# The last expert's rows of both routed MoE layers are added to the stream by a product on TensorE instead of a scatter and a read-back

## The reference

```python
# x (1, 512, 1024) behind 16 meta tokens: 528 rows of a stream h
h = h + short_conv_mixer(rmsnorm(h, a_norm), a_w_in, a_conv, a_w_out)
h = h + hier_moe(rmsnorm(h, ffn_norm[0]), ...)          # MoE layer 0, 528 rows
kv = rmsnorm(h, kv_norm) @ w_kv                         # keys and values from the stream
h = h[:, 16:]
h = h + diff_attention(rmsnorm(h, b_norm), ...)
h = h + hier_moe(rmsnorm(h, ffn_norm[1]), ...)          # MoE layer 1, 512 rows
return rmsnorm(h, final_norm)
# hier_moe: 32 experts in 4 groups; a row takes the 2 best experts of its best group
#   y = sum over the two: gate_k * (silu(x @ w_gate[e]) * (x @ w_up[e])) @ w_down[e]
```

## Time and profile before

| | us |
|---|---|
| median of 3 runs | 1638.5 |
| lowest, highest | 1637.38, 1640.2 |
| the profiled execution: its own time | 1636.99 |
| its span, first to last instruction | 1635.2 |

### The profile page before, as it was taken

How to read it: one execution, slowest core, us unless ns; L and a number is a source line. 1 busy time by engine, 2 the same in 40 slices (tenths; PEclk the granted TensorE clock), 3 DMA queues, 4 the chain that set the end, 5 groups by cost and what they waited for, 6 DMA issues and landing times. The chain is left out here.

```text
span 1635.2 us, 17518 instructions
## 1 busy us (share of the span) xinstructions
PE 1361.8 (83%) x6689; PEld 755.3 (46%) x6689; DVE 378.6 (23%) x729; ACT 341.0 (21%) x625; POOL 190.1 (12%) x314
## 2 busy tenths in 40 slices
PE   5999994999888888875999978895999888888882
PEld 4999772333322322233676755783333322323230
DVE  3434423000000000004431388623000000000003
ACT  5222220101000000004544366331010000000002
POOL 2000000111111111111000000001112111111111
PEclk9999995999999999997999979996999999999996
DMA  9120417999999999995312110317999999999994
GB/s 342 44 104 1 167 75 315 415 425 425 425 427 426 424 425 426 426 416 180 111 52 103 52 52 1 155 57 304 415 425 425 425 426 427 423 426 423 424 382 165
DMA packets 60922, 472.67 MB, mean 289 GB/s; under 512 B 10592, under 2 KB 10668, under 8 KB 35776
## 3 DMA queue, kind: packets, MB, share of 16 engines
q1 hardware_dynamic: 46480, 441.48, 65.2%
q0 software_dynamic: 14384, 30.36, 5.0%
HBM read 465.17 MB, written 23.13 MB: 299 GB/s over the span
## 5 line engine op out<-in xcount | busy, mean ns | idle before, releaser
L943 PE MATMUL ps<-ring,act 128*64 128x512 f32 x1792 | 443.8, 649 | 74.7 <-DMA ring<-in_e_up 68.8
L943 PEld LDWEIGHTS ps<-ring,act 128*64 128x64 f32 x1792 | 139.9, 142 | 373.9 <-issue 373.9
L910 PE MATMUL ps<-parts 128*128 128x512 f32 (+1 forms) x1104 | 265.1, 398 | 8.3 <-DVE parts L1220 7.7
L966 PE MATMUL ps<-ring,act 128*64 128x512 f32 x896 | 204.6, 597 | 31.0 <-ACT act L763 31.0
L1403 DVE TENSOR_TENSOR act<-act,ps 128x256 f32<-128x256 f32 x64 | 26.9, 421 | 870.1 <-ACT act L761 870.1
L910 PEld LDWEIGHTS ps<-parts 128*128 128x128 f32 (+1 forms) x1104 | 194.0, 178 | 69.1 <-DVE parts L1220 5.9
L896 PE MATMUL ps<-parts 128*128 128x264 f32 x1152 | 143.6, 287 | 4.5 <-DVE parts L1215 2.9
L896 PEld LDWEIGHTS ps<-parts 128*128 128x128 f32 x1152 | 142.3, 190 | 5.5 <-issue 5.5
L761 ACT ACTIVATE act<-ps 128x256 f32<-128x256 f32 x64 | 24.6, 384 | 574.3 <-PE ps L943 574.3
L966 PEld LDWEIGHTS ps<-ring,act 128*64 128x64 f32 x896 | 70.8, 136 | 126.2 <-issue 126.2
L1215 DVE TENSOR_TENSOR parts<-ring,parts 128x1024 fp32r<-128x1024 f32 x64 | 77.8, 1224 | 117.6 <-ACT parts L694 117.4
(11 more groups left out here) (163 smaller groups left out, 880.8 us busy)
## 6 DMA issues: line engine op xcount, KB each, us to landing
ring<-in_e_gate SPq DMA_DIRECT2D x56, 2048.0 KB, 18.2
ring<-in_e_up SPq DMA_DIRECT2D x56, 2048.0 KB, 22.5
ring<-in_e_down SPq DMA_DIRECT2D x56, 2048.0 KB, 22.4
arena<-in_e_down SPq DMA_DIRECT2D x8, 2048.0 KB, 15.6
ring<-in_a_w_in SPq DMA_DIRECT2D x6, 2048.0 KB, 19.6
arena<-in_e_up SPq DMA_DIRECT2D x6, 2048.0 KB
arena<-in_e_gate SPq DMA_DIRECT2D x6, 2048.0 KB
ring<-in_w_kv SPq DMA_DIRECT2D x4, 2048.0 KB, 13.2
```

What stands on the lines that cost most here:

```text
L910: last = mm(bank, x[:, k, :], w[:, k, :], start=(k == 0 and i == 0), stop=(k == KC - 1 and i == 2))
L943: last = mm(ps[f * C:(f + 1) * C, 2 + b, :].rearrange("p (g m i) -> p g m i", g=2, i=2), x, w, start=(k == 0), stop=(k == KC - 1))
L966: last = mm(ps[o * C:(o + 1) * C, 6 + b, :], hT[:, b, (2 * c + a) * C:(2 * c + a + 1) * C], w[:, f * D + o * DH:f * D + (o + 1) * DH], sta ...
```

## The change

The rows of expert 31 are no longer scattered and read back. After routing, DVE multiplies the slot marks of choices 0 and 1 by gate and by "this choice is expert 31", adds the two, and writes the 64 columns twice side by side (`hot_gate`). PE transposes that, DVE copies it into a free half of `nat`. ACT copies the last expert's result to `last_y` (two halves of the columns, on partitions 0 to 63 and 64 to 127). For each tile, PE multiplies the marks by the result (`add_last`, two products of 64 rows by 512 columns), and DVE adds the result to h (`take_last`). As no scatter writes those places of `expert_rows`, POOL fills all of them with zeros early in the kernel. The part for further blocks moves ahead of the last expert on every engine, and so does the read-back. ACT's squares of the two later norms are written elsewhere, as `nat` is occupied.

```diff
+        hot_gate = act17[:, 3584:4224].rearrange("p (t a n) -> p t a n", t=NX + 1, a=2)
+        def last_gate(t):
+            return nat[:, 0, DH + t * P:DH + (t + 1) * P] if t < NX else nat[:, 1, DH:DH + META]
+        def last_rows(layer, t):
+            b = 2 * (t % 2) if layer == 0 else 2 * t
+            return ps[0:rows(t), b:b + 2, :]
+        last_y = nat[:, 0, 0:DH]
+        def squares(phase, t):
+            return y_in(min(t, NX - 1), 0)[0:rows(t), :] if phase in (2, 4) else nat[0:rows(t), t % 2, :]
...
 POOL, start
+            nc.gpsimd.memset(zero, 0.0).then_inc(zero_ready, 1)
+            pool.wait_ge(zero_ready, 1)
+            pool.wait_ge(in_done, 6)
+            for l in range(2):
+                for k in range(2):
+                    for t in range(NX):
+                        pool.dma_start(y_dram[l][k * SPREAD + t * P:k * SPREAD + (t + 1) * P, :].rearrange("p (a n) -> p a n", a=2),
+                                       bcast(zero, 2, 1)).then_inc(zeroed, 16)
...
+            pool.wait_ge(zeroed, 16 * (4 * NX + 2))
 POOL, moe
+                        if last and u == 1:
+                            continue
                         pool.wait_ge(y_ready, E * layer + q * 2 + u + 1)
...
                 for b in range(2):
-                    pool.wait_ge(scattered[layer][b], 16 * PAIRS)
+                    pool.wait_ge(scattered[layer][b], 16 * (PAIRS - b))
 ACT, moe: pair(q, early) becomes one(q, u, early, final=False) for u in 0, 1
-                        if not first:
+                    if not first and not final:
                             act.wait_ge(scattered[layer][u], q * 16)
-                        nc.scalar.copy(y_out[:, u, :], ps[:, 6 + u, :]).then_inc(y_ready, 1)
+                    nc.scalar.copy(last_y if final else y_out[:, u, :], ps[:, 6 + u, :]).then_inc(y_ready, 1)
...
-                with act.Fori(EARLY, PAIRS) as q:
+                with act.Fori(EARLY, PAIRS - 1) as q:
                     pair(q, False)
+                one(PAIRS - 1, 0, False)
                 more = load_more(act, layer)
                 with act.If(more > 0):
...
+                one(PAIRS - 1, 1, False, True)
 PE, moe
+                pe.wait_ge(last_marked, layer + 1)
+                for t in range(nt):
+                    r = rows(t)
+                    at = ps[:, 4, t * P:(t + 1) * P] if t < NX else ps[:, 5, 0:META]
+                    last = nc.tensor.transpose(at, hot_gate[0:r, t, :, :].rearrange("p a n -> p (a n)"), ident[0:r, 0:r])
+                last.then_inc(last_turned, 1)
                 pe.wait_ge(gathered[layer][0], 16)
                 turn_block(0).then_inc(x_turned, 1)
...
-                pair(PAIRS - 1, False, True)
+                one(PAIRS - 1, 0, False, True)
                 more = load_more(pe, layer)
                 with pe.If(more > 0):
...
+                one(PAIRS - 1, 1, False, True)
 PE, after the layers
+            def add_last(layer, t):
+                pe.wait_ge(y_ready, E * (layer + 1))
+                for a in range(2):
+                    last = mm(last_rows(layer, t)[:, a, :], last_gate(t)[a * C:(a + 1) * C, :], last_y[a * C:(a + 1) * C, :], start=True, stop=True)
+                last.then_inc(last_done, 1)
...
-            turn_stream(0)
-            turn_stream(1)
+            for t in range(2):
+                add_last(0, t)
+            for t in range(2):
+                turn_stream(t)
             nrot = 0
             for p in range(len(JOBS)):
+                if p + 2 <= NX:
+                    pe.wait_ge(act_low_ready, T_KVQ + p + 1)
+                    add_last(0, p + 2)
                 project(p)
...
             moe(1)
+            for t in range(NX):
+                add_last(1, t)
 DVE, moe, behind row_numbers
+                sel = rv[:, 12:14, 0:nt]
+                order(v.tensor_tensor(sel, ch.rearrange("p (k t) e -> p k t e", k=2)[:, :, :, E - 1], gate[:, :, 0:nt], ALU.mult))
+                slots = at_slot[:, 0:2 * nt, :].rearrange("p (k t) n -> p k t n", k=2)
+                for k in range(2):
+                    order(v.tensor_tensor(slots[:, k], slots[:, k], bcast(sel[:, k], C, 2), ALU.mult))
+                v.tensor_tensor(hot_gate[:, 0:nt], bcast(slots[:, 0], 2, 2), bcast(slots[:, 1], 2, 2), ALU.add).then_inc(last_marked, 1)
+                for b in range(2):
+                    dve.wait_ge(hn_stored[layer][b], 16 * ((nt + 1 - b) // 2))
+                dve.wait_ge(last_turned, layer + 1)
+                order(v.tensor_copy(nat[:, 0, DH:D], ps[:, 4, :]))
+                if nt > NX:
+                    order(v.tensor_copy(last_gate(NX), ps[:, 5, 0:META]))
...
 DVE, after the layers
+            def take_last(layer, t):
+                r = rows(t)
+                dve.wait_ge(last_done, (NX + 1) * layer + t + 1)
+                v.tensor_tensor(h[0:r, t, :], h[0:r, t, :], last_rows(layer, t).rearrange("p b n -> p (b n)"), ALU.add).then_inc(combined[layer], 1)
...
             combine(0, 0)
             for t in range(NX + 1):
+                take_last(0, t)
                 if t < NX:
                     combine(0, t + 1)
                 act_low(T_KVQ + t)
                 rstd_tile(2, t)
...
             combine(1, 0)
             for t in range(NX):
+                take_last(1, t)
                 if t + 1 < NX:
                     combine(1, t + 1)
```

More of the change, by code:

```diff
@@ L654, in root_mean_square @@
                 r = rows(t)
-                step.order(nc.scalar.activation(nat[0:r, t % 2, :], h[0:r, t, :], ACT.Square, scale=1.0 / math.sqrt(D),
+                step.order(nc.scalar.activation(squares(phase, t), h[0:r, t, :], ACT.Square, scale=1.0 / math.sqrt(D),
                                                 accum_out=ssq[0:r, t:t + 1]))
@@ L752, in moe, with one @@
                         nc.scalar.activation(lam[:, 2:4], lam[:, 0:2], ACT.Exp).then_inc(lam_exp, 1)
+                def one(q, u, early, final=False):
+                    lead, first = early and 2 * q + u in LEAD, early and q == 0
+                    if lead:
+                        act.wait_ge(lead_used, lead_done(layer, 2 * q + u) + 1)
+                    else:
+                        act.wait_ge(unit_used, ring_uses(layer, q, u, early) + 2)
+                    nc.scalar.activation(silu[:, u, :], ps[:, 2 + u, 0:FE // 2], ACT.Silu).then_inc(silu_ready, 1)
+                    act.wait_ge(hidden_turned, E * layer + q * 2 + u + 1)
+                    nc.scalar.copy(hT[:, u, :], ps[:, 4 + u, 0:FE // 2]).then_inc(hT_ready, 1)
+                    if lead:
+                        act.wait_ge(lead_used, lead_done(layer, 2 * q + u) + 2)
+                    else:
+                        act.wait_ge(unit_used, ring_uses(layer, q, u, early) + 3)
+                    if not first and not final:
+                        act.wait_ge(scattered[layer][u], q * 16)
+                    nc.scalar.copy(last_y if final else y_out[:, u, :], ps[:, 6 + u, :]).then_inc(y_ready, 1)
@@ L754, in pair @@
                 def pair(q, early):
                     for u in range(2):
-                        lead, first = early and 2 * q + u in LEAD, early and q == 0
-                        if lead:
-                            act.wait_ge(lead_used, lead_done(layer, 2 * q + u) + 1)
-                        else:
-                            act.wait_ge(unit_used, ring_uses(layer, q, u, early) + 2)
-                        nc.scalar.activation(silu[:, u, :], ps[:, 2 + u, 0:FE // 2], ACT.Silu).then_inc(silu_ready, 1)
@@ new lines, in one @@
+                def one(q, u, early, last_pair):
+                    lead, first = early and 2 * q + u in LEAD, early and q == 0
+                    (gs, gv), (us, uv), (ds, dv) = (expert_unit(layer, q, u, part, early) for part in ORDER)
+                    if lead:
+                        pe.wait_ge(lead_landed, lead_landing(layer, 2 * q + u))
+                        pe.wait_ge(xT_ready, E * layer + q * 2 + u + 1)
+                        gate_up(u, lead_w, lead_half_used if first else None).then_inc(lead_used, 1)
+                    else:
+                        pe.wait_ge(ring_landed[gs], gv)
+                        pe.wait_ge(ring_landed[us], uv)
+                        pe.wait_ge(xT_ready, E * layer + q * 2 + u + 1)
+                        gate_up(u, ring[:, gs:us + 1, :]).then_inc(unit_used, 2)
+                    if not (last_pair and u == 1):
+                        pe.wait_ge(gathered[layer][1 - u], q * 16 + 16 * (1 + u))
+                        turn_block(1 - u).then_inc(x_turned, 1)
+                    pe.wait_ge(hidden_ready, E * layer + q * 2 + u + 1)
+                    turn_hidden(u).then_inc(hidden_turned, 1)
+                    if lead:
+                        pe.wait_ge(lead_down_landed, 16 * (len(LEAD) * layer + LEAD.index(2 * q + u) + 1))
+                    else:
+                        pe.wait_ge(ring_landed[ds], dv)
+                    if not first:
```

(20 more changed lines are left out.)

54 lines of the change are left out of this document (13 added, 41 removed).

## The result

| | median us | runs | ratio to the kernel before on the same chip (95%) |
|---|---|---|---|
| before | 1639.31 | 6 | |
| changed | 1648.97 | 6 | 1.0064 (1.0047 to 1.008) |

What follows compares the result with a forecast made beforehand. DMA streaming expert weights was taken to set the pace in two long stretches, other things at their ends. Handover 9.0, tail -4.7, start -1.0 gave +3.3 us: 1641.9 predicted, 1639.5 to 1644.5, 8-of-10 range 1638.0 to 1646.0.

Steps and rivals of the forecast that it cites:

- the move of the part for further blocks on PE: Register load and jump on PE between the last two experts, load under expert 30's product: 0, at most 0.6 us.
- The handover: From layer 0's last expert to tile 4's transposition: 9.0 us lost, from added DVE additions, PE pairs and low clock.
- Tile 0: Handover: transposed at 762.4 instead of 761.64, 0.5 us gained on ACT and 1.25 lost to the added addition.
- Tile 1 behind tile 0: Handover: tile 1's addition waits on DVE behind tile 0's reciprocal, so tile 1 is transposed 4.4 us later than before.
- rival 4: DVE's order costs less, tile 1 not held by the table load, both ends gain: -3.2 us, 1638.7; chance 0.10.
- The two pairs between tile 2 and tile 4: Handover: two added pairs of products in PE's unbroken run, 1.0 to 1.2 us each, 2.2 us lost.
- The tail: End of layer 1: scatter, release and read-back leave the path, products and additions join it; 21.9 against 26.6, 4.7 us gained.
- rival 1: Products of the two halves run one after the other, in tail and handover: +3.5 us, 1645.4; chance 0.12.
- The start of the experts: New DVE work hidden; PE's new transpositions raise the clock earlier: 1.0 us gained in layer 1, 0 in layer 0.
- Rival 2: New transpositions bring the high clock to both layers' first expert, releases 2.3 us earlier each: 1638.2; chance 0.15.
- rival 3: POOL's gathers held 1.6 us per layer by DVE's work in SBUF at the experts' start: +3.2 us, 1645.1; chance 0.08.
- The zeros: 18 DMAs, 8.5 MB, during the first projection while DMA is idle: 0, at most 1 us.

Runs made afterwards that it cites:

- load_only: Changed kernel with PE keeping the register load of the number of further blocks, without the jump and the part behind it; 1641.11 us, one run.
- layer1_only: Product in place of scatter and read-back in layer 1 alone, layer 0 as in the kernel before; 1636.32 us, ratio 0.9972 to the kernel before.
- no_jump: Changed kernel with PE's part for further blocks left out, register load and jump included; 1643.53 us, ratio 1.0021 to the kernel before.
- after_loop: Changed kernel with the table products of the further blocks written as a loop on PE; 1643.07 us, ratio 1.0014 to the kernel before.
- changed, again: The changed kernel run and traced once more, code unchanged; 1649.89 us, ratio 1.0074 to the kernel before.

## Why the prediction was wrong, step by step

**The failed step** is the move of the part for further blocks on PE: "I take 0, at most the 0.6 us that the same step left open on ACT". It cost 6.5 us (4.6 in layer 0, 1.9 in layer 1). I priced the register load, found it under expert 30's down product, and that was right: load_only costs nothing. I did not price the jump over the unrolled part. From the register load to the next product pass 6.5 to 9.1 us where the jump holds it, and the wait for the weights covers 3.8 to 5.8. In the old order the load of layer 0 ran at 743.7, and PE's next work is at 761.64, 18 us later, and behind layer 1 nothing follows: there the jump is hidden. But its price stood in the trace of the kernel before, 4.53 and 3.29 us, and I didn't ask for it. It was a bound from below only. From load to the end of the jump that is 5.6 and 4.0 us, which the wait for the weights would have covered but for 0 to 2 us a layer; in the new place the jump takes 4.9 to 8.1 us in the ten cases, against 3.3 to 4.5 in the six in the old place. The 0.6 us on ACT was no bound: ACT's jump goes over its own part and takes 0.05 us.

**The handover**, +9.0 predicted, +8.2 measured (counted from ACT's last copy; over all traces with this order 46.3 to 47.1 us, in those with layer 0 as before 37.6 to 38.7): right.
- Tile 0 0.75 predicted, 0.57 measured (766.02 - 751.70 against 761.64 - 747.89).
- Tile 1 behind tile 0 by 3.65 more predicted (4.4 - 0.75), 3.51 measured, behind the reciprocal as named; rival 4 is out.
- Tile 2 behind tile 1 by 2.4 predicted, 1.7 measured: the pair took 2.08 at the low clock (774.97), but less of the first projection was left for that clock, 5.94 us instead of 6.55.
- The two pairs between tile 2 and tile 4: 2.2 predicted, 2.4 measured, 1.2 each (their records are 1.13 and 1.03 long) where a pair in a row of four takes 0.93. "TensorEngine Tiling (Array Packing)" of the Trainium skill, Key Properties, says that a change of tiling mode drains TensorE. The trace leaves at most 0.3 us a pair for that and doesn't show that it is a drain: the first pair of the tail, behind an idle engine, is 1.15 long as well.

**The tail**, -4.7 predicted, -5.2 measured: right. Only the first pair is on the path, and it is 1.15 (1.2 predicted); the 0.5 is mostly the pace of the later tiles, 5.16 us in place of 5.3. In the single records of a pair the products of the two halves start 5 to 8 ns apart, so the halves overlap and rival 1 is out. The read-back starts 3.3 us later than predicted, as the weights still stream in under it, and is hidden all the same.

**The start of the experts**, -1.0 predicted, 0 measured: wrong by 1 us. From row numbers to the first release it takes 12.62 and 13.31 us in the two profiles of the kernel before, and 12.04 to 13.48 in all with the new transpositions. The clock rose no earlier: at 1152.7 in the changed kernel, 12.2 us behind the row numbers (1140.55), and at 1137.0 in the kernel before, 10.9 behind them; in all traces it is 9.7 to 12.2 with and 10.4 to 12.1 without the new transpositions. So the reading that PE's first piece of work would count for the rise didn't hold here. Rival 2 is out, as is the 3.2 us of rival 3. POOL was slowed all the same. Timeline of POOL at the start of layer 1, before and after:

```profile
1126.45 0.18 POOL L586 COPY src_now<-src_row 128x1 uint32<-128x1 uint32 x1 [21.06 <-DVE src_row L1387]
1127.56 1.12 POOL L589 DMA_INDIRECT nat<-hn_rows,src_now  x1 [0.93 <-POOL src_now L586]
```

```profile
1140.90 0.41 POOL L619 COPY src_now<-src_row 128x1 uint32<-128x1 uint32 x1 [20.48 <-DVE src_row L1452]
1142.24 1.21 POOL L622 DMA_INDIRECT nat<-hn_rows,src_now  x1 [0.93 <-POOL src_now L619]
```

The copy takes 0.41 instead of 0.18 and the issue 1.21 instead of 1.12, while DVE multiplies in SBUF: 0.3 us where rival 3 had 1.6. In layer 0 it is 0.5 (0.49 and 1.36 for 0.19 and 1.12). In layer1_only the copy is 0.19 in layer 0 and 0.42 in layer 1, so it goes with the change; that the two engines get in each other's way is argued from this.

**The zeros**, 0 predicted: right. They ran from 66.45 on, and PE stands at the same distance to the profile of before (0.74 us) ahead of them and at 167. A kernel without them was not tried.

**Sum.** Without the jump the steps give 9.0 - 4.7 - 1.0 = +3.3; no_jump and after_loop measured +3.4 and +2.3. The sum was right for a kernel without that step, in part by luck: handover and tail came out 1.3 us better than predicted, and the 1.0 of the start didn't come. (Two small slips in the working: the median by its own terms is 1638.5 + 3.3 = 1641.8, and the terms of the start add up to 3.8, not 3.9. Neither bears on the outcome. The 7.5 given as lower end of the handover isn't worked out there.)

## What stays open

Why the jump over the long part takes so long. That code has to be fetched behind it is not shown by an experiment, but the traces point there. Each of the 16 long jumps has a 16 KB packet of the page's instruction queue (q8) in its time, none of the eight short ones (empty body or loop, 0.21 to 0.36 us) has. For the jump of layer 0 in the changed kernel, DMA in the window 731.61:737.77 reads:

```profile
q8 instruction: 1, 0.02, 1.0%
```

From the start of that packet to the end of the jump it is 2.3 to 2.6 us in the 14 cases with one packet (of the two with two packets, 3.6 to 4.1), in the old place and the new. What differs is the time ahead of the packet: 0.5 to 1.5 us in the old place, where DMA moves 4 to 7 GB/s, and 2.3 to 5.7 in the new one, where it moves 144 to 381. So the jump is longer where the expert weights stream in. That the packet waits behind them is the plain reading, and no run here varies it.

Nor is it settled from what length on a part costs; only a loop and an empty instruction were tried against the unrolled one. The later start and the low clock behind it are not separated either: the clock was low in 7 of 10 products behind the long jump, which is a count and not a cause. And the sum of parts is below the measured loss of the changed kernel (9.5 against 10.5 and 12.1), within the intervals.

## What to carry to other kernels

A jump over a long unrolled part that costs nothing where the engine idles for 18 us behind it costs several where it has 5: before a step is moved, look up how long the branch itself took in the old place (4.53 and 3.29 us here, in a sequencer's row that a timeline leaves out), set it against the cover in the new one, and allow for more where DMA is busy: here it grew to 4.9 to 8.1. If the part is rarely run, write it as a loop; that alone took back 8 us here (10.5 less 2.3). And count a moved wait from the landing of what the engine waits for anyway, not from the start of the gap.

## What the hardware showed that I had not expected

- The jump itself: a COMPARE_BRANCH of 4.9 to 8.1 us on PE over the unrolled part while weights stream in, 3.3 to 4.5 with DMA idle, 0.33 to 0.36 over the loop and 0.21 over an empty body. From the register load to the next product it is 6.5 to 9.1 us; one of the ten cases was done within 5.8 (changed, again, layer 1), where the weights came last. With the loop, an empty body or the load alone the product starts 0.1 us behind the landing of its weights, at most 5.7 us behind that load.
- Two products of 64 rows by 512 columns in fp32 on the two halves of the partitions take 0.93 us together at full clock (3.70 for four pairs), less per column (0.91 ns) than the 1.18 ns of the first pair in the earlier trace rows; a pair that stands alone is 1.13 to 1.15 long.
- The product behind the gap takes 7.42 us in some executions and 8.7 to 10.2 in others, at a mean granted clock down to 0.7. It was the longer in seven cases with a gap of 3.4 to 5.6 us ahead and in three with 2.1 to 2.2, and 7.42 behind gaps of 2.97 and 3.65 and all others. So one and the same kernel differs by several us at that place.
